# A two-block transformer on one core: modulation products, PSUM bank rotation, a root and a table load in other places

## The reference

```python
# block 1
h = rmsnorm(x, attn_norm_w)
qkv_la, z_la, b_la, a_la, q_d, k_d, v_d = split(h @ w_in)
o_la = gated_delta_rule(silu(causal_conv(qkv_la)), ...)       # 4 heads, chunks of 64
o_la = rmsnorm(o_la, la_norm_w) * silu(z_la)
o_d  = rmsnorm(softmax(q1 k1) v - lam * softmax(q2 k2) v)     # 4 heads, 2 maps each
x = x + concat(o_la, o_d) @ w_out
x = x + (silu(gate) * up) @ w_down                            # of rmsnorm(x)
x = rmsnorm(x, final_norm_w)
# block 2
mod = silu(c) @ w_ada + b_ada                                 # 1024 x 6144, one row
h = rms_norm(x) * (1 + sc_m) + sh_m
y = (sigmoid(gate_a) * attention(h) + sigmoid(gate_b) * conv31(glu(h))) @ w_mix_o
x = x + gt_m * rms_norm(y)
x = x + gt_f * rms_norm(conv_ffn(rms_norm(x) * (1 + sc_f) + sh_f))
```

## Time and profile before

| | |
|---|---|
| median of 3 executions | 787.25 us (785.51, 787.54, 787.25) |
| the profiled execution | 787.85 us, span of its instructions 786.1 us |
| TensorE busy | 755.4 us, 96% of the span |
| VectorE busy | 573.5 us, 73% |
| ScalarE busy | 391.0 us, 50% |
| GpSimd busy | 26.7 us, 3% |
| mean granted TensorE clock | 0.992 |
| weights and other reads | 147.02 MB, 188 GB/s over the span |

### The profile page before, as it was taken

One profiled execution on the slowest core, in us unless ns is written; L12 is line 12 of the kernel. 1 busy time (PEld: TensorE's weight loads), 2 busy tenths in 40 slices (PEclk: granted clock), 3 DMA queues, 4 the chain that ended last, 5 costly groups with the idle time before them and its releaser, 6 DMA issues.

```text
span 786.1 us, 13349 instructions
## 1 busy us (share of the span) xinstructions
PE 755.4 (96%) x5290; PEld 694.9 (88%) x5290; DVE 573.5 (73%) x963; ACT 391.0 (50%) x661; POOL 26.7 (3%) x32
## 2 busy tenths in 40 slices
PE   7999999779999999999999999999999999999996
PEld 7988999777899999999979887798979999999995
DVE  5748889866766776678677998766766766766776
ACT  5472323554544443444474454557357555555554
POOL 0030000100000000000013000000000000000000
PEclk9999999999999999999999999999999999999999
DMA  7733355643289978889706532364434665565431
GB/s 292 260 95 102 108 174 176 199 150 123 93 299 388 336 272 276 285 290 348 261 35 203 186 106 92 123 213 160 139 134 161 205 201 186 164 211 188 162 135 53
DMA packets 40526, 148.94 MB, mean 189 GB/s; under 512 B 4496, under 2 KB 4624, under 8 KB 40080
## 3 DMA queue, kind: packets, MB, share of 16 engines
q1 hardware_dynamic: 39600, 142.91, 53.0%
q10 hardware_dynamic: 864, 5.18, 1.7%
HBM read 147.02 MB, written 1.05 MB: 188 GB/s over the span
## 4 chain that ended last, share of the span: by engine, by line
PE 75%; DVE 14%; ACT 6%; issue 2%; DMA 1%; POOL 0%; DVEq 0%; SPq 0%; ACTq 0%
PE bank L1030 13%; PE bank L1031 13%; PE bank L1033 13%; PE bank L1071 6%; PE bank L1072 6%; PE bank L1069 6%; PE bank L1047 5%; PE bank L1196 4%; DVE wlo L1426 3%; DVE arena L1432 3%; PE bank L1060 3%; DVE XN L1432 2%; DVE arena L1426 2%; ACT whi L1972 2%; ACT XN L1972 2%
## 5 line engine op out<-in xcount | busy, mean ns | idle before, releaser
L1030 PE MATMUL bank<-hh,whi 128*128 128x256 f32 x1008 | 289.9, 288 | 0.7 <-DVE hl L1426 0.5
L1031 PE MATMUL bank<-hl,whi 128*128 128x256 f32 x1008 | 286.1, 284 | 0.0
L1033 PE MATMUL bank<-hh,wlo 128*128 128x256 f32 x1008 | 286.0, 284 | 0.0
L1426 DVE TENSOR_TENSOR wlo<-raw,whi 128x1024 fp32r<-128x1024 f32 x202 | 242.1, 1231 | 26.0 <-ACT whi L1972 25.8
L1972 ACT ACTIVATE whi<-raw 128x1024 fp32r<-128x1024 f32 x202 | 202.3, 1047 | 31.9 <-DMA raw<-w_dram 21.8
L1030 PEld LDWEIGHTS bank<-hh,whi 128*128 128x128 f32 x1008 | 194.2, 193 | 5.0 <-issue 2.9
L1031 PEld LDWEIGHTS bank<-hl,whi 128*128 128x128 f32 x1008 | 194.3, 193 | 1.5
L1033 PEld LDWEIGHTS bank<-hh,wlo 128*128 128x128 f32 x1008 | 194.1, 193 | 0.0
L1432 DVE SCALAR_TENSOR_TENSOR arena<-bank,cols,arena 128x255 f32<-128x255 f32 (+3 forms) x138 | 58.9, 480 | 32.0 <-ACT arena L1972 27.8
L1972 ACT ACTIVATE arena<-bank 128x256 f32<-128x256 f32 (+2 forms) x65 | 26.9, 422 | 94.1 <-PE bank L1033 70.2
L1071 PE MATMUL bank<-wlo,fh 128*128 128x512 f32 x176 | 69.1, 393 | 1.1 <-DVE wlo L1426 1.1
(11 more groups left out here) (169 smaller groups left out, 890.3 us busy)
## 6 DMA issues: line engine op xcount, KB each, us to landing
raw<-w_dram SPq DMA_DIRECT2D x268, 512.0 KB, 4.8
arena<-rows_dram ACTq DMA_DIRECT2D x1, 1792.0 KB, 9.6
X<-x_dram SPq DMA_DIRECT2D x2, 512.0 KB, 4.7
arena<-rows_dram ACTq DMA_DIRECT2D x1, 1024.0 KB, 13.0
arena<-bias_dram ACTq DMA_DIRECT2D x1, 1024.0 KB, 16.3
out_dram<-X SPq DMA_DIRECT2D x4, 256.0 KB, 2.1
const<-const_dram ACTq DMA_DIRECT2D x1, 640.0 KB, 3.8
arena<-bias_dram ACTq DMA_DIRECT2D x1, 512.0 KB, 4.9
```

Source lines behind the costliest of these rows:

```text
L1030: e.matmul(o, a, hh[:, k, :], start=(k == 0), stop=False)
L1031: e.matmul(o, a, hl[:, k, :], start=False, stop=False)
L1033: ins = e.matmul(o, wlo[:, s, k * 128:k * 128 + 128], hh[:, k, :], start=False, stop=(k == 7))
L1426: return e.tensor_tensor(out, a, b, op)
```

## The change

- `stream`: of the 16 early modulation products, four are taken from behind matmul units 22 to 24 (`w_in_qk` 3 and 7, `w_in_z` 0) and put behind units 9 to 11 (`w_in_qk` 4, `w_in_v` 0 and 1), near the gates. The others move by a place or two.
- `delta`: the bank of `o0` is released from the hold after `la_rows(0)`, while that of `o1` stays held until `oT1` has its bank. The rotation of the side banks up to the output projection comes out differently.
- `P.lag` is set to False ahead of the `w_out` units, and ahead of `u2` in the second block, where one unit more is prepared before the step.
- `stats` moves from GpSimd's power to ScalarE's square root and a reciprocal on VectorE. `keep(5)` is removed.
- `pair(first=True)` makes a new step `front` of the first unit of norms 1 and 2: all eight products of the high half of the activations come first, and then the four with the low half.
- `mod01` is filled in bank 4. In the last block, `root` stands ahead of `pre`, and a new step `table` (a table load for the square root and one dummy root) stands ahead of the matmuls of the last four `w_down_2` units.

```diff
--- before.py
+++ after.py
-        for _ in range((16 <= n < 28) + (n in (18, 20, 22, 24))):
+        for _ in range((9 <= n < 12 or 16 <= n < 28 and n not in (23, 24)) + (n in (10, 18, 20))):
             out.append(early.pop(0))
...
-            P.step("stat" if kind == "s" else "whole", i, 0)
+            P.step("front" if first and n == 0 else "stat" if kind == "s" else "whole", i, 0)
...
         for n, b in enumerate((2, 3, P.main % 2, (P.main + 1) % 2)):
             P.fill(f"wo{n // 2}{n % 2}", b)
+        P.lag = False
         for k in range(4):
...
         P.step("la_rows", 0)
+        P.held.discard(held[0])
         yield
...
         P.step("la_rows", 1)
-        P.held.difference_update(held)
         yield
-        held = P.take(hold=True)
+        last = P.take(hold=True)
+        P.held.discard(held[1])
         P.fill("oT0")
-        P.fill("oT1", held)
+        P.fill("oT1", last)
         P.step("turn_la")
...
         P.step("spread_od")
-        P.keep(5)
...
+        if first:
+            P.step(first)
         last_four(norm_next, f"d{n}", down, range(FT - 4, FT), f"f{n}", block)
...
-    P.fill("mod01", (P.main + 1) % 2)
+    P.fill("mod01", 4)
...
-        P.prepare(P.prepared + 1)
+        P.lag = False
+        P.prepare(P.prepared + 2)
         P.step("u2")
...
     def out2_block(b):
+        P.step("root", b)
         P.step("pre", 1, b, 0)
-        P.step("root", b)
         P.step("pre", 1, b, 1)
...
-    ffn(2, None, "w_up_2", "w_down_2", 3, None, out2_block, None)
+    ffn(2, None, "w_up_2", "w_down_2", 3, None, out2_block, "table")
...
+            def front(i, _):
...
+                for k in range(4):
+                    c = slice(k * 128, k * 128 + 128)
+                    e.matmul(o, whi[:, s, c], hh[:, k, :], start=(k == 0), stop=False)
+                    e.matmul(o, wlo[:, s, c], hh[:, k, :], start=False, stop=False)
+                h_ready(norm, 0)
+                for k in range(4):
+                    e.matmul(o, whi[:, s, k * 128:k * 128 + 128], hl[:, k, :], start=False, stop=False)
...
+                e.reciprocal(rst, rst).then_inc(sems["rinv"], 1)
+                w.wait_ge("rinv", 1)
                 tt(rst, rst, fits, ALU.mult).then_inc(sems["fits"], 1)
...
+            def stats():
+                wait_after("rs_od")
+                af(rst, rst, ACT.Sqrt).then_inc(sems["rstat"], 1)
+
+            def table():
+
+                w.wait_ge("pconst", 2)
+                af(rq_[:, 13:14], de, ACT.Sqrt)
...
-            def stats():
-                wait_after("rs_od")
-                tt(rst, rst, pw[:, 0:8], ALU.pow).then_inc(sems["rstat"], 1)
```

More of the change, by code:

```diff
@@ L260, in plan, with pair @@
     flags = set()
-    def pair(tag, name, fs, src, kind="s"):
+    def pair(tag, name, fs, src, kind="s", first=False):
         bank = P.main % 2
@@ L289, in first_four @@
     def first_four(norm, tags, name, fs):
-        finish(pair(tags[0], name, fs[0:2], ("h", norm)))
+        finish(pair(tags[0], name, fs[0:2], ("h", norm), first=True))
         if norm == 2:
@@ L511, in delta @@
         P.step("head_la", 1)
-        P.held.discard(held)
+        P.held.discard(last)
         flags.add(("la", 1))
@@ L802 @@
 pconst sq ssum rpow xnd xna h_hi h_lo xw sc gt wb wbl csilu cva cvd qkv b1m lam gate gate_act dsq rnorm em atri
-um0 ym rd sqv rstat fits hv osq oms orpow ofac mixh_od mixl_od mixh_la mixl_la mxn pexp prec pn pscale sm
+um0 ym rd sqv rstat rinv fits hv osq oms orpow ofac mixh_od mixl_od mixh_la mixl_la mxn pexp prec pn pscale sm
 sg fh1 fl1 ga gd gg gm fh2 fl2 biases2 gl_t gl_s pad b2m tap cen csq rs lnv lns u2h u2l
@@ L1035, in stat @@
                     done(i, ins)
+            def front(i, _):
+                tag, n, (_, norm) = P.of[i]
+                s = place[i] % HL
+                o = open_bank(tag)[:, 0:256]
+                w.wait_ge("hi", place[i] + 1)
+                w.wait_ge(*P.lo_on[i])
+                for t in (2 * norm, 2 * norm + 1):
+                    w.wait_ge("h_hi", P.hi_at[t, 0])
+                for k in range(4):
[5 more added lines that the diff above has]
+                    e.matmul(o, whi[:, s, k * 128:k * 128 + 128], hl[:, k, :], start=False, stop=False)
             def whole(i, part):
@@ L1398, in _ @@
             does = {
-                "start": start, "turn": turn, "stat": stat, "whole": whole, "half": half, "movv": movv, "mov": mov, "four": four, "ba": ba,
+                "start": start, "turn": turn, "stat": stat, "front": front, "whole": whole, "half": half, "movv": movv, "mov": mov, "four": four, "ba": ba,
                 "turn_ba": turn_ba, "lam": lam_, "norms": norms, "decay": decay, "kk": kk, "kq": kq, "lev_first": lev_first,
@@ L2290, in _ @@
                 "conv": conv, "silu": silu, "lam": lam_, "vd": vd_, "qk": qk, "z": z, "gates": gates, "dsq": dsq, "decay": decay,
-                "solve": solve, "values_la": values_la, "head_la": head_la, "spread_od": spread_od, "head": head, "scores1": scores1, "soft1": soft1, "turn1": turn1,
+                "solve": solve, "values_la": values_la, "head_la": head_la, "stats": stats, "table": table, "spread_od": spread_od, "head": head, "scores1": scores1, "soft1": soft1, "turn1": turn1,
                 "values1": values1, "scores2": scores2, "soft2": soft2, "turn2": turn2, "values2": values2, "tables": tables,
@@ L2374, in _ @@
                 "start": start, "prep": prep, "sums": sumsq, "sumsq": sumsq, "ba": ba, "factors": factors, "decay": decay,
-                "la_sums": la_sums, "stats": stats, "gate_mul": gate_mul,
+                "la_sums": la_sums, "gate_mul": gate_mul,
                 "biases2": biases2, "mask2": mask2,
```

## The result

| | before | changed |
|---|---|---|
| median of 4 executions each | 786.38 us | 779.72 us |
| lowest to highest | 785.38 to 787.54 | 778.70 to 780.76 |
| the profiled execution | 787.85 us, span 786.1 | 779.02 us, span 777.2 |

The ratio is 0.9915, with a 95% interval of 0.9891 to 0.9938. The changed kernel is faster by 6.7 us (4.9 to 8.6). I had forecast 783.7 and a range down to 780.7: right in sign, half the size.

The account below looks back on a forecast made before the run. The prediction took TensorE, busy 96% of the span, as the bound, so only gaps and clock losses could be won. Its terms summed to 3.5 us, giving 784.35 for the profiled execution and a median of 783.7, range 780.7 to 786.7.

Parts of the forecast that it names:

- products gone, 143 us: First block's attention: moving modulation products away lets scores and solve start earlier, gain 1.5 us, bounds 0.2 and 3.0.
- bank rotation, 165 us: Values matmul no longer waits for VectorE's bank; gain 2.7 us less 0.9 for the clock: 1.8, bounds 1.2 and 2.7.
- output projection: Earlier low halves, no fill, root on ScalarE: 0.87 + 1.28 us less 0.6 becoming visible, 1.55, bounds 0.9 and 2.1.
- hand-over: Start of the feed-forward part: waits of 0.78 and 0.49 us go, gain 1.2 of 1.27.
- norm 2: Feed-forward start at norm 2, where the prediction had no term of its own: 0.
- convolution: Second block: a high half moves ahead of the activations, an early low half repays part; -0.4 us, bounds -1.1 and 0.
- tail: Table load and dummy root delay the last unit by 1.57 us, 0.87 given back, perhaps a clock fall: -1.4.
- gates: 50 to 54 us: three products in VectorE's queue collide with GpSimd's spreads, softmax late; -0.75 us, bounds -1.6 and 0.
- the clock that stays up: Rival: no clock fall behind the gaps at 143 and 165 us, 781.3; one fall gone, about 782.5; chance 0.22.
- The other two: Rivals: next landing holds ScalarE at 143 us, 785.6 to 786.6, chance 0.22; late landing at gates, 790 or more, 0.06.
- my anchor: Starting point for the whole kernel: median of 787.25 us before, 0.6 under the profiled execution's 787.85.
- the price of the clock: Half-level clock falls assumed behind the transpose at 165 us (0.9 us) and in the tail (up to 1.7 more).

Follow-up runs that it names:

- e5: The changed kernel without the step that loads the table and takes a dummy root before the last unit; 778.65 us, ratio 0.99 to the kernel before.
- e11: The changed kernel with the head norms' root as GpSimd's power again and the ten fill matmuls back; 781.20 us, ratio 0.9917 to the kernel before.
- e10: The changed kernel with the first unit of norms 1 and 2 in its old order, without the front; 780.19 us, ratio 0.991 to the kernel before.
- e12: e8 with the two steps of the root in the final norm in their old order; 775.61 us, ratio 0.9863 to the kernel before.
- e6: The changed kernel with the table load and dummy root moved behind the last unit's high half; 777.84 us, ratio 0.9885 to the kernel before.
- e9: The changed kernel itself, unedited, timed and profiled once more; 778.29 us, ratio 0.9893 to the kernel before.
- e1: The kernel before with the four modulation products moved alone; 784.61 us, ratio 0.997.
- e8: The changed kernel with the table load behind the last high half and the convolution's preparation as before; 776.41 us, ratio 0.9874 to the kernel before.
- e2: The kernel before with the bank rotation of the delta rule alone; 782.71 us, ratio 0.9946.

## Why the prediction was too careful

Term by term, forecast and what the traces of the changed kernel show:

| term | forecast | measured |
|---|---|---|
| products gone, 143 us | 1.5 | 1.94 |
| bank rotation, 165 us | 1.8 | 2.64 |
| output projection | 1.55 | 1.95 |
| hand-over | 1.2 | 1.81 |
| norm 2 | 0 | 0.13 |
| convolution | -0.4 | -0.4 |
| tail | -1.4 | -0.4 |
| gates | -0.75 | -0.36 |
| sum | 3.5 | 7.3 |

**The mechanisms were as forecast.** Each wait went, moved or grew where the prediction said: 2.44 for "about 2.4", 0.41 and 1.98 for "0.3 and then 2 us", 0.97 and 0.70 for "0.8 and 0.9". Of the rivals, the clock that stays up came about in one of its two places, at 165 us. The other two did not: no landing held ScalarE at 143 us, and none held the gates. With one fall gone my number was about 782.5; that the time lies 2.8 us under this too comes from the other terms and from my anchor.

**The step that failed first is the price of the clock.** The prediction says that "the clock, which fell just before the projection, can now fall behind the transpose", and takes 0.9 for it. It takes another 0.7 in the tail. The sizes were right: e5 pays 1.0 and e11 1.6 when it happens. What failed is the argument from one place that a stand of 1.68 us "was enough". It was enough at the convolution of the kernel before, nearly always, but not everywhere: behind such stands the clock fell in 5 of 8 traces at the convolution, and in 1 of 10 and 1 of 5 at the two places that I charged. Neither fall happened in the two traces of the changed kernel, and with 0.84 in the bank term and 0.7 in the tail that makes 1.5 us of the 3.8 that were missing. As share times cost the two would have been 0.1 and 0.3, though five traces tell a share only roughly. At 143 us, where I left the fall as it was, it did stay in 7 of 10. Why the clock falls behind one such stand and not behind another stays open.

**The second is that waits were counted at their brackets.** The wait of 0.78 at the modulation gave 0.90, that of 0.49 gave 0.72 (e10 agrees, with nothing else changed), that of 0.87 between 1.0 and 1.15. A matmul of the earlier trace rows reads 0.35 us where its like elsewhere read 0.28, and in a full stream like ones start 0.12 apart though each lasts 0.28. So I read a stand as costing its bracket, plus the overlap that the last matmul before it would have had (0.28 - 0.12 = 0.16), plus a slower first one behind it (0.07). For the wait of 0.49 that is 0.72, as measured; the wait of 0.12 at norm 2 gave 0.13 to 0.14, which this does not explain. The spread came 0.96 earlier, where I had left 0.6 of the sum to "what becomes visible". Together the projection and the hand-over were 1.0 us too low. Of the 1.94 at 143 us, 0.28 are won at 129.73, where a wait of 0.12 on ScalarE went: I had left it out.

**The third is the tail's repayment.** I gave 0.87 for the load that leaves the final chain and the earlier root; it is 1.1, most of the load's 1.28, and the root has no part in it (e12). The cost ahead of the last unit was 1.52 against my 1.57. The net loss of 0.4 is real (e5), and the load's place behind the high half has the gain without it (e6). That a load is followed at once by the next instruction held again: 765.10 to 766.39 in e6. By the figure in the Trainium skill's "ScalarE: Activation LUTs", section "What ACT_TABLE_LOAD costs", a drain of some 1.38 us comes on top of the load; the trace shows none, neither ahead of the load (the high half ends at 765.09) nor behind it.

**The gates** cost 0.36 and not 0.75. VectorE's timeline of the changed kernel:

```profile
48.38 3.27 DVE L1453 SCALAR_TENSOR_TENSOR arena<-raw,small,arena 128x1024 f32<-128x1024 f32 x2
51.57 2.06 DVE L1447 TENSOR_TENSOR wlo<-raw,whi 128x1024 fp32r<-128x1024 f32 x1
53.55 0.16 DVE L1450 TENSOR_SCALAR small<-bank 128x16 f32<-128x16 f32 x1
...
56.45 0.45 DVE L1447 TENSOR_TENSOR small<-small 128x8 f32<-128x8 f32 x3 [0.40 <-POOL small L2340]
...
57.95 0.28 DVE L1775 CUSTOM_DVE_ANT_0 arena<-bank,arena 128x128 f32<-128x128 f32 x1
```

```profile
48.60 3.94 POOL L2340 TENSOR_TENSOR arena<-const,small 128x512 f32<-128x512 f32 x2 [26.63 <-DVE small L1453]
```

The second fence has GpSimd's two spreads, the first VectorE's rows. While the spreads run, the two products take 3.27 us in place of 2 x 1.28, and the low half behind them 2.06 in place of 1.22. The page "SBUF — State Buffer" of the Trainium skill (section "SBUF: two separate sides") has such operations lock each other out, and I chose its side; the longer times agree with that, though the rows do not show the turns themselves. But in the time of the trace before, which is 1.57 later, the norms' read is at 55.1, the softmax at 59.5 instead of 58.96, 0.56 late, and TensorE at 69.88 is 0.36 late. The chain behind the softmax took up 0.2 of it; where, I did not follow.

**Against the medians.** The traces give 7.3 us; the medians give 6.7, and e9's pair 7.9. The interval of the 6.7, 4.9 to 8.6, holds all three. My anchor, the median of three at 787.25, also stood 0.9 over the median that the kernel before has with four (786.38).

## What to carry to other kernels

Price a fall of the clock as its share times its cost, with the share from several traces of this very kernel, and not as a certainty from another place; the mean clock of each execution tells how many falls it had. Compare two kernels by the start of the same instruction in both traces, so that the falls can be told from the change. Count a TensorE wait of 0.5 to 0.9 us as its bracket and 0.1 to 0.3 us more; one of 0.12 was worth no more than that. Before a table load is moved ahead, look for the idle time of ScalarE that lies behind the last work for others: here the same load cost 1.5 us on one side of a weight unit and nothing on the other.

## What the runs showed of the hardware

- The first matmuls run at half pace until a moment that differs between executions (11.7 us in the trace before, 8.2 in e1, which by then is 1.9 us ahead). The clock's first record comes at that moment; the granted clock of 1.00 that the view gives for the time before it stands for no record.
- One kernel with the same stands falls in clock in some executions and not in others, and its time scatters in steps: e11 took 781.1 to 781.3 four times and 778.5 to 778.9 twice, e10 780.2 to 781.0 three times and 778.2 to 778.3 twice, each at mean clocks of 0.995 and 0.996. That the tail's fall makes e11's steps is likely, but only one execution of each was profiled.
- A half-clock stretch cost 1.2 us at 143 us (e8 against e9: 2.13 to 3.33 and 2.74 to 2.74 between 144.52 and 156.00), 1.0 at 165 us in e5, 1.5 behind the convolution (e2), and 1.6 in the tail (e11).
